# One pass over all tokens instead of two, with feature-major activations, in an eight-core decoder-trunk kernel

## The chip, the cores and the metric

The kernel runs on all 8 NeuronCores of one Trainium2 chip. Every core executes the same program on its own slice of the tokens, and the cores exchange nothing. The metric is device time in microseconds (us) of the slowest core, as the median of several executions.

## What is computed

Four layers of a hybrid decoder trunk, for a prompt of 4 x 2048 tokens and a sample group of 128 x 8 tokens. The width is 2048, and the feed-forward width 8192.

```python
def _layer(x, pool_hist, conv_hist, pos0, ...):
    proj = jnp.einsum('bld,de->ble', x, w_in)          # 2048 -> 4096
    p, u, v, gate_b, gate_c, z = jnp.split(proj, IN_SPLITS, axis=-1)
    a_out, pool_new = _pool_mixer(p, pool_hist, pos0, w_pool, pool_scale)  # trailing windows 2/4/8/16
    u = jax.nn.gelu(u)
    v = _layernorm(jax.nn.gelu(v), ln_v_g, ln_v_b)
    b_out = _spatial_gate(u, v, w_s, b_s)              # 8 heads, 128-position chunks
    conv_y, conv_new = _short_conv(gate_c * z, conv_hist, w_conv)          # width 3
    mix = jnp.concatenate([a_out, b_out, gate_b * conv_y], axis=-1)
    h = _layernorm(ALPHA * x + jnp.einsum('ble,ed->bld', mix, w_out), ln1_g, ln1_b)
    f = jnp.einsum('blf,fd->bld', jnp.square(jax.nn.relu(h @ w_ff1)), w_ff2)
    x = _layernorm(ALPHA * h + f, ln2_g, ln2_b)
```

Per token and layer the four large weight matrices hold 512 (w_in), 256 (w_out), 1024 (w_ff1) and 1024 (w_ff2) blocks of 128 x 128, together 2816. All inputs and outputs are float32 in HBM; the matmuls run in bf16.

## The kernel before

Each core owns half a sequence (1024 prompt tokens) and 128 sample tokens. A sequence is divided between two cores at position 1024, and pooling, convolution and gating look back, so a core that has a second half also computes tokens ahead of its own, which get fewer from layer to layer. The tokens are worked in tiles of 128 and in **two passes of six tiles** (`T = 768` columns). Pass 0 holds three tiles of such lead-in and three own tiles, pass 1 five own tiles and the sample tile. In pass 0 the output tiles shrink to 6, 5, 4 and 3 in layers 0 to 3. Both passes go through all four layers, so all weights are read twice, in 2 x 4 x 44 = 352 blocks of 2048 x 512 (2 MB as bf16 in SBUF). There are two slots (`wsl0`, `wsl1`). GpSimd's queue starts a block's transfer when the slot's last reader on TensorE is done, and the transfer converts fp32 to bf16.

The residual `X` stands token-major in SBUF (tokens on partitions), in fp32. A layer runs through `phase_v`, `phase_b`, `phase_a`, `phase_c`, `phase_out` and `phase_ffn`:

- Projections whose result is wanted feature-major take weights as the stationary operand and `actT` as the moving one, in groups of 256 to 512 columns (384 with six tiles). Projections that return to `X` (`w_out`, `w_ff2`, also `v`) take 128 tokens as the stationary operand and 512 weight columns as the moving one.
- ScalarE evicts the first half of the feed-forward (`relu2`: Relu into `rl`, then Square into `mixT`). VectorE adds the second half to `X`, line 352 or 362.
- A layernorm is done per tile of tokens (`ln_stats`, `ln_rstd`, `ln_apply`): `bn_stats` on four pieces of 512, then two passes of 2048 on VectorE (L362). `fm_cast` (ScalarE) makes a bf16 copy `xb`, and `fm_tr` transposes it on TensorE into `ptb` (L451), from where ScalarE copies it to `actT`. The next projection needs `actT`.
- Matmuls rotate over six PSUM banks `pb` and two banks `ptb` for transposes. Engines run in program order, and every wait is on a semaphore.

Line 340 of the profile is the helper `mm` (every matmul), 349 `act`, 352 `tt`, 356 `ts`, 362 `stt`, 99 `dma`. The loop of the feed-forward that carries most of the work reads:

```python
            for s in range(4):
                for fb in range(4):
                    ...
                    sl, sbf = w_get()
                    for e in range(4):
                        for gi in range(ngrp):
                            ...
                                mm(pt[:, 0:gw], sl[:, dc, e * 128:(e + 1) * 128], actT[:, dc, c0:c1], ...
                            relu2(mixT[:, fc, c0:c1], pt[:, 0:gw], gw, pb, mixbufs(fc, c0, c1))
                for db in range(4):
                    sl, sbf = w_get()
                    for t in tiles:
                            mm(pt[:, :], mixT[:, fc, t * 128:(t + 1) * 128], sl[:, fc, :], fc == 0, fc == 15, ...
```

## Time and profile before

| what | value |
|---|---|
| time, median of 3 runs | 8297.62 us (8265.32 to 8550.75) |
| span of the profiled execution, slowest core | 8170.0 us |
| spans of the eight cores | 8077.3 to 8170.0 us |
| TensorE busy | 6971.1 us (85%), 39048 matmuls |
| VectorE / ScalarE busy | 1810.8 us (22%) / 1655.2 us (20%) |
| HBM read | 1542.85 MB |

The span goes from the first to the last instruction on the core. The times of the runs hold what lies around it too; the profiled execution has no time of its own beside its span. The lowest of the three runs lies 95 us above this span and the median 128 us. A row on the clock gives the share of its full speed (2.4 GHz) that TensorE was granted, as a mean over a stretch.

### The profile page before, as it was taken

What the parts mean: (1) busy time and instruction counts of PE and PEld (TensorE: products, weight loads), DVE (VectorE), ACT (ScalarE), POOL (GpSimd) and SP (SyncE); (2) the same over time, 40 slices, a digit from 0 to 9 for tenths busy, and PEclk for the clock granted to TensorE, in tenths of its full rate; (3) what the DMA queues carried; (4) which work ended last, traced back from release to release, by engine and by line L of the source; (5) the groups of instructions that cost most, each with busy time, mean ns of one, the idle gap of its engine ahead of it and who ended that gap; (6) DMA issues with size and microseconds to landing.
All of it is one profiled execution on the core that took longest, in us unless ns stands there. A gap on an engine that the chain in (4) does not pass through costs nothing.

```text
span 8170.0 us, 94139 instructions; the slowest of 8 cores (8077.3 to 8170.0 us)
## 1 busy us (share of the span) xinstructions
PE 6971.1 (85%) x39048; PEld 3714.9 (45%) x39048; DVE 1810.8 (22%) x2667; ACT 1655.2 (20%) x2864; POOL 420.0 (5%) x377
## 2 busy tenths in 40 slices
PE   6899977999788866676889987899978999788998
PEld 3455544555443333333455544555434555345454
DVE  2410143101320041003320033311234100432112
ACT  3122120221211121113021221211131222212111
POOL 0000000000000000000000000000000000000000
PEclk9899988999899988888899988999989999889999
DMA  5566655788489869996567644667736788546775
GB/s 101 93 101 101 100 87 94 111 112 116 79 134 120 125 97 134 117 121 131 88 94 103 97 77 72 113 97 103 94 65 98 93 96 101 81 80 98 98 99 103
DMA packets 761119, 822.23 MB, mean 101 GB/s; under 512 B 26740, under 2 KB 748148, under 8 KB 753852
## 3 DMA queue, kind: packets, MB, share of 16 engines
q0 software_dynamic: 743264, 742.43, 65.8%
q1 hardware_dynamic: 17436, 73.77, 2.6%
q8 instruction: 317, 5.19, 0.3%
q14 instruction: 102, 0.84, 0.0%
HBM read 1542.85 MB, written 16.65 MB: 191 GB/s over the span
## 4 chain that ended last, share of the span: by engine, by line
PE 66%; DMA 19%; DVE 7%; issue 5%; ACT 3%; DVEq 0%; another core or an unknown queue 0%; ACTq 0%; POOL 0%; POOLq 0%; SPq 0%
PE pb L340 65%; DMA wsl<-w_ff 14%; DMA wsl<-w_in 3%; DVE X L362 3%; DMA wsl<-w_out 2%; DVE R L352 1%; DVE stats L424 1%; PE ptb L451 1%; ACT actT L349 1%; DVE R L362 1%; ACT L349 1%; ACT R L349 0%; ACT xb_0 L349 0%; ACT xb_1 L349 0%; DVE stats L409 0%
## 5 line engine op out<-in xcount | busy, mean ns | idle before, releaser
L340 PE MATMUL pb<-actT,wsl 128*128 128x384 bf16 (+3 forms) x21696 | 3446.9, 323 | 376.0 <-DMA wsl<-w_ff 261.5
L340 PE MATMUL pb<-wsl,mixT 128*128 128x512 bf16 x13440 | 2936.2, 381 | 106.0 <-DMA wsl<-w_ff 67.7
L340 PEld LDWEIGHTS pb<-actT,wsl 128*128 128x128 bf16 x21696 | 2061.6, 101 | 1736.3 <-issue 571.8
L340 PEld LDWEIGHTS pb<-wsl,mixT 128*128 128x128 bf16 x13440 | 1318.1, 98 | 1714.4 <-issue 155.3
L349 ACT ACTIVATE rl<-pb 128x384 f32<-128x384 f32 (+3 forms) x1008 | 456.7, 453 | 3411.8 <-PE pb L340 3411.6
L352 DVE TENSOR_TENSOR X<-pb,X 128x512 f32<-128x512 f32 x504 | 347.9, 690 | 3401.7 <-PE pb L340 3401.6
L362 DVE SCALAR_TENSOR_TENSOR X<-X,pb 128x512 f32<-128x512 f32 x336 | 230.4, 686 | 1533.8 <-PE pb L340 1533.5
L99 POOL DMA_DIRECT2D wsl<-w_ff x256 | 292.7, 1143 | 5021.6 <-PE pb L340 5001.4
L349 ACT ACTIVATE mixT<-rl 128x384 bf16<-128x384 f32 (+3 forms) x1008 | 491.9, 488 | 96.8 <-ACT rl L349 5.9
L362 DVE SCALAR_TENSOR_TENSOR X<-X,mvall,R 128x2048 f32<-128x2048 f32 x168 | 389.9, 2347 | 12.3 <-DVE mvall L433 2.9
L340 PE MATMUL pb<-wsl,actT 128*128 128x512 bf16 x1344 | 310.5, 395 | 42.6 <-DMA wsl<-w_in 42.6
L349 ACT ACT_TABLE_LOAD x100 | 128.3, 1283 | 1038.1 <-DVE mvall L426 926.2
L451 PE MATMUL ptb<-identb,xb_1 128*128 128x128 bf16 x720 | 77.4, 278 | 233.6 <-ACT actT L349 188.4
L340 PEld LDWEIGHTS pb<-wsl,actT 128*128 128x128 bf16 x1344 | 135.7, 101 | 214.4 <-issue 69.0
L424 DVE BATCH_NORM_STATS2 stats<-X 128x6 f32<-128x512 f32 x336 | 206.8, 678 | 0.0
L451 PE MATMUL ptb<-identb,xb_0 128*128 128x128 bf16 x672 | 66.7, 270 | 155.4 <-ACT xb_0 L349 94.6
L340 PE MATMUL pb<-dd,wpool_t 128*128 128x384 bf16 (+2 forms) x56 | 22.6, 492 | 203.4 <-DVE dd L362 110.0
L349 ACT ACTIVATE R<-pb 128x384 f32<-128x384 f32 (+2 forms) x204 | 109.1, 535 | 428.4 <-PE pb L340 424.9
L349 ACT ACTIVATE actT<-ptb 128x1024 bf16<-128x1024 bf16 x174 | 176.9, 1017 | 24.1 <-PE ptb L451 15.0
L451 PEld LDWEIGHTS ptb<-identb,xb_1 128*128 128x128 bf16 x720 | 61.3, 125 | 249.1 <-issue 249.0
L99 POOL DMA_DIRECT2D wsl<-w_in x64 | 73.4, 1147 | 1831.5 <-PE pb L340 1831.5
L349 ACT ACTIVATE mvall<-mvall,epst 128x3 f32<-128x3 f32 (+2 forms) x30 | 9.0, 300 | 660.3 <-DVE mvall L426 660.2
(70 smaller groups left out, 1435.5 us busy)
## 6 DMA issues: line engine op xcount, KB each, us to landing
wsl<-w_ff POOLq DMA_DIRECT2D x256, 2048.0 KB, 17.2
wsl<-w_in POOLq DMA_DIRECT2D x64, 2048.0 KB, 15.7
wsl<-w_out POOLq DMA_DIRECT2D x32, 2048.0 KB, 16.8
R<-ln_g SPq DMA_DIRECT2D x16, 1024.0 KB, 5.3
R<-ln_b SPq DMA_DIRECT2D x16, 1024.0 KB, 7.4
X<-x_in SPq DMA_DIRECT2D x12, 1024.0 KB, 18.1
y<-X SPq DMA_DIRECT2D x9, 1024.0 KB, 3.9
R<-lnv_g SPq DMA_DIRECT2D x8, 512.0 KB, 4.3
```

The lines of the kernel that those rows point to most:

```text
L99: q.h.dma_start(out=out, in_=in_).then_inc(ds.sem, 16)
L340: return op(PE, lambda: nc.tensor.matmul(out, lhsT, rhs, start=start, stop=stop), reads=reads, writes=[bank], acc=not first, force_inc=boo ...
L349: return op(ACT, lambda: nc.scalar.activation(out=out, in_=in_, func=func, **kw), reads=reads, writes=writes)
L352: return op(DVE, lambda: nc.vector.tensor_tensor(out=out, in0=in0, in1=in1, op=o), reads=reads, writes=writes)
L362: return op(DVE, lambda: nc.vector.scalar_tensor_tensor(out=out, in0=in0, scalar=scalar, in1=in1, op0=o0, op1=o1), reads=reads, writes=writes)
L424: op(DVE, lambda k=k: nc.vector.bn_stats(out=st[:, k, :], in_=X[:, t, k * 512:(k + 1) * 512]), reads=[Xb[t][k]], writes=[stb[k]])
L451: op(PE, lambda k=k, dc=dc, pt=pt: nc.tensor.transpose(pt[:, k, :], xb[:, dc * 128:(dc + 1) * 128], identb[:]), reads=[xbb, identbb], writ ...
```

## The change

The kernel is written anew around the same arithmetic.

- **One pass.** A core holds 1296 columns at once: 16 + 112 lead-in columns, 16 columns `E` (the first 16 positions of a sequence's second half, or those just before), 1024 own and 128 sample columns. Layer 0 computes 1280 of them to the end, layers 1 to 3 compute 1168 (`O_START`). The sequence is now divided at position 1040, 16 positions inside a 128-position chunk, and small extra operations handle those 16 (`before_e`, `WE`, `CBE`, `et`, `ey`).
- **Weights** are read once, in 4 x 176 = 704 blocks of 2048 x 128, stored contiguously in HBM by the host, through ten slots of one buffer `wsl` (`w_issue` after a block's last use).
- **Features on partitions throughout.** `X`, the activations `actg[g]` and `mixT` are feature-major; weights are always the stationary operand (save for `v`), and each block is applied to three token groups `g` = 2, 1, 0 of 512, 384 and 272 columns (384 in layer 0). There are no transposes. All eight PSUM banks rotate.
- **Layernorm by token groups.** While the last projection before a layernorm is evicted, `stat_acc` adds each of the 16 feature chunks to `sacc` (VectorE) and its square (ScalarE) to `qacc` (VectorE). `ln_stats` sums both over the partitions by two fp32 matmuls with a matrix of 1/2048, then computes Ln and Exp on ScalarE for the reciprocal root. 16 `items` per group (VectorE `scale`, `shift`, ScalarE gain and offset into bf16) apply it. `tail` runs the last eight blocks group by group and interleaves the items of the group before, and `head` runs the first eight blocks of the next projection group by group while the rest is applied. Gain and offset of `X` itself are not applied but folded into the next residual (`aga`).
- **SBUF** doesn't hold everything at once: mixer buffers lie in the space of `X`, which is written to HBM after the second layernorm (`xs_d`) and read back before `w_out` (`reload`, 8 transfers).
- **Input** comes feature-major in fp32, in four transfers per token group, each group after the one before, and ScalarE and VectorE convert it.

```diff
-NT = 6
-T = NT * 128
-TG = 384
 ALPHA = (2 * DEPTH) ** 0.25
 EPS = 1e-5
 WINDOWS = (2, 4, 8, 16)
-NSLOT = 2
+TIN = 1296
+XO = 16
+TX = TIN - XO
+C_T, C_E, C_OWN, C_S = 16, 128, 144, 1168
+P_START = (0, 112, 128, 128)
+O_START = (16, 128, 128, 128)
+GB = ((0, 400), (400, 784), (784, 1296))
+ORDER = (2, 1, 0)
+NWB = 176
+NSLOT = 10
...
-        def w_issue_upto(k):
-            while wstate['issue'] <= min(k, len(blocks) - 1):
-                b = wstate['issue']
-                s = b % NSLOT
-                dma(POOL, wsl[s][:], blocks[b], wsld[s], writes=[wslb[s]])
-                wstate['issue'] += 1
-
-        def w_get(hold=0):
-            b = wstate['use']
-            w_issue_upto(b + NSLOT - 1 - hold)
-            wstate['use'] += 1
-            return wsl[b % NSLOT], wslb[b % NSLOT]
-
...
-        def ln_stats(t):
-            i = ln_rot.next()
-            st, stb = stats[i], statb[i]
-            for k in range(4):
-                op(DVE, lambda k=k: nc.vector.bn_stats(out=st[:, k, :], in_=X[:, t, k * 512:(k + 1) * 512]),
-                   reads=[Xb[t][k]], writes=[stb[k]])
-            op(DVE, lambda: nc.vector.bn_aggr(out=mvall[:, t, 0:2], in_=st[:, 0:4, :].rearrange("p k s -> p (k s)")),
-               reads=stb[0:4], writes=[mvallb[t]])
-
...
-                pt, pb = ptp.next()
-                for k in range(8):
-                    dc = half * 8 + k
-                    op(PE, lambda k=k, dc=dc, pt=pt: nc.tensor.transpose(pt[:, k, :], xb[:, dc * 128:(dc + 1) * 128], identb[:]),
-                       reads=[xbb, identbb], writes=[pb], acc=(k > 0), force_inc=(k == 7))
-                act(actT[:, half * 8:(half + 1) * 8, t * 128:(t + 1) * 128], pt[:, :, :], AF.Copy, [pb], [actb[t]])
...
+        def w_issue():
+            b = wst['issue']
+            if b >= nblk:
+                return
+            s = b % NSLOT
+            dma(POOL, wsl[:, s].rearrange("p a b -> p (a b)"), wb_d[b], wds[s], writes=[wsl[:, s]])
+            wst['issue'] += 1
...
+        def fm4(places, c0, c1):
+
+            got = [banks.next() for _ in range(4)]
+            for k in range(16):
+                for i, (pt, bk) in enumerate(got):
+                    lw, rh = wsl[:, places[i], k, :], actc(k, c0, c1)
+                    mm(pt[:, 0:c1 - c0], lw, rh, k == 0, k == 15, [lw, rh], bk, k == 0)
+            return got
...
+        xin_ds = [[dsem(f"xin{g}_{q}") for q in range(4)] for g in range(3)]
+        for g in ORDER:
+            if g < 2:
+                SP.wait_for(('d', xin_ds[g + 1][3], 16))
+            for q in range(4):
+                d = xst[g][:, 4 * q:4 * q + 4, :]
+                dma(SP, d, xg_d[g][:, 4 * q:4 * q + 4, :], xin_ds[g][q], writes=[d])
...
+            if off is None:
+                tt(s_, x, s_, ALU.add, [x, s_], [s_])
+            else:
+                stt(s_, x, off, s_, ALU.add, ALU.add, [x, s_] + ro, [s_])
+            q_flush()
+            sq = sqt[g].next()[:, 0:n]
+            act(sq, x, AF.Square, [x] + ro, [sq], bias=off)
+            pend.append((q, sq))
...
+        def ln_stats(g, c0, c1):
+            n = c1 - c0
+            s_, q = sacc[g][:, 0:n], qacc[g][:, 0:n]
+            pm, bm = banks.next()
+            mm(pm[:, 0:n], onesf[:], s_, True, True, [onesf[:], s_], bm, True)
+            pq, bq = banks.next()
+            mm(pq[:, 0:n], onesf[:], q, True, True, [onesf[:], q], bq, True)
+            a, b = rn[g][0][:, 0:n], rn[g][1][:, 0:n]
+            m2 = sqt[g].next()[:, 0:n]
+            act(m2, pm[:, 0:n], AF.Square, [bm], [m2])
+            act(a, pm[:, 0:n], AF.Copy, [bm], [a])
+            tt(b, pq[:, 0:n], m2, ALU.subtract, [bq, m2], [b])
+            ts(b, b, 0.0, None, ALU.max, None, [b], [b])
+            act(b, b, AF.Ln, [b, epst[:, 0:1]], [b], bias=epst[:, 0:1], scale=1.0)
+            act(b, b, AF.Exp, [b], [b], scale=-0.5)
+            stt(a, a, -1.0, b, ALU.mult, ALU.mult, [a, b], [a])
+
...
+                def scale():
+                    if off is None:
+                        tt(x, x, b, ALU.mult, [x, b], [x])
+                    else:
+                        o_ = off(c)
+                        stt(x, x, o_, b, ALU.add, ALU.mult, [x, b, o_], [x])
+
+                def shift():
+                    tt(x, x, a, ALU.add, [x, a], [x])
+                    gg, bb = vec(l, gi + c), vec(l, bi + c)
+                    if after == 'y':
+                        act(x, x, AF.Identity, [x, gg, bb], [x], scale=gg, bias=bb)
+                    else:
+                        h = actc(c, c0, c1)
+                        act(h, x, AF.Identity, [x, gg, bb], [h], scale=gg, bias=bb)
...
+        def tail(og, src, ks, resid, accum, items, rate=(1, 1, 2), order=ORDER):
+
+            places = [w_get() for _ in range(8)]
+            prev = None
+            for gi, g in enumerate(order):
+                c0, c1 = og[g]
+                for i in range(8):
+                    pt, bk = fm(places[i], c0, c1, src, ks)
+                    if gi == 2:
+                        w_issue()
+                    now = [todo.pop(0) for _ in range(min(rate[gi], len(todo)))]
+                    for scale, _ in now:
+                        scale()
+                    resid(8 + i, g, c0, c1, pt, bk)
+                    for _, shift in now:
+                        shift()
+                    accum(8 + i, g, c0, c1)
+                    if prev is not None and i == 2:
+                        p0, p1 = og[prev]
+                        ln_stats(prev, p0, p1)
+                        todo.extend(items(prev, p0, p1))
+                q_flush()
+                prev = g
+            return prev
...
+        def head(og, sink, last, items):
+            places = [w_get() for _ in range(8)]
+            for gi, g in enumerate(ORDER):
+                c0, c1 = og[g]
+                if last is not None:
+                    drain(len(todo) - (16 if gi < 2 else 0))
+                if gi < 2:
+                    for i, (pt, bk) in enumerate(fm4(places, c0, c1)):
+                        sink(i, c0, c1, pt, bk)
+                if last is not None:
+                    drain(6)
+                for i in range(4 if gi < 2 else 0, 8):
+                    if last is not None:
+                        if gi == 0 and i == 6:
+                            p0, p1 = items[1][last]
+                            ln_stats(last, p0, p1)
+                            todo.extend(items[0](last, p0, p1))
+                        drain(3)
+                    pt, bk = fm(places[i], c0, c1, actc, K16)
+                    if gi == 2:
+                        w_issue()
+                    sink(i, c0, c1, pt, bk)
...
+            work = [lambda h=h: b_head(l, h) for h in range(8)]
+            work[3:3] = [lambda g=g: pool_map(l, g) for g in range(4)]
+            work.pop(0)()
...
+                for e in (2 * half, 2 * half + 1):
+                    for block in (c_gate, c_z):
+                        block(l, e, w_get())
+                        w_issue()
+                        work.pop(0)()
+                for j in range(2):
+                    c_out(l, 2 * half + j, w_get())
+                    w_issue()
+                    if work:
+                        work.pop(0)()
+            dma(SP, ctail_d[l], ctail[:], dd["ct_o"], reads=[ctail[:]])
...
+            for e in range(8):
+                s = w_get()
+                for g in ORDER:
+                    c0, c1 = og[g]
+                    pt, bk = fm(s, c0, c1, mixc, KW)
+                    out_resid(e, g, c0, c1, pt, bk)
+                    out_accum(e, g, c0, c1)
...
```

Three places show what stands in a row now. On TensorE, at the end of `w_out` and the start of the feed-forward in pass 0, layer 0, before (`pb<-wsl,mixT` is `w_out`, `ptb` are transposes of layernormed tiles, `pb<-actT,wsl` the first block of `w_ff1`):

```order
L340 MATMUL pb<-wsl,mixT 128x512 x384
L451 MATMUL ptb<-identb,xb_0 128x128 x16
L451 MATMUL ptb<-identb,xb_1 128x128 x16
L340 MATMUL pb<-actT,wsl 128x128 x64
L451 MATMUL ptb<-identb,xb_0 128x128 x16
L340 MATMUL pb<-actT,wsl 128x128 x64
```

And the same place now, on TensorE in layer 1 (`act_44`, `act_45`, `act_46` are the activations of groups 2, 1 and 0; `onesf` marks the two sums of `ln_stats`):

```order
L343 MATMUL pb<-mixT,wsl 128x512 x128
L343 MATMUL pb<-mixT,wsl 128x384 x48
L343 MATMUL pb<-sacc_101,onesf 128x512
L343 MATMUL pb<-qacc_102,onesf 128x512
L343 MATMUL pb<-mixT,wsl 128x384 x80
L343 MATMUL pb<-mixT,wsl 128x272 x48
L343 MATMUL pb<-sacc_103,onesf 128x384
L343 MATMUL pb<-qacc_104,onesf 128x384
L343 MATMUL pb<-mixT,wsl 128x272 x80
L343 MATMUL pb<-act_44,wsl 128x512 x96
```

The transposes and the 128-column matmuls between them are gone. The sums of a group stand three blocks behind its last matmul.

On VectorE in the third group of the same `tail` (`rnB`, `rnA` are scale and shift of group 2, `agab` the folded gain, `rnD`, `rnC` those of group 1), now:

```order
L336 SCALAR_TENSOR_TENSOR X<-X,agab,rnB 128x512 x2
L336 SCALAR_TENSOR_TENSOR X<-X,agab,pb 128x272
L327 TENSOR_TENSOR X<-X,rnA 128x512 x2
L336 SCALAR_TENSOR_TENSOR sacc_105<-X,agab,sacc_105 128x272
L327 TENSOR_TENSOR qacc_106<-qacc_106,sqt_109 128x272
L327 TENSOR_TENSOR rnD<-pb,sqt_108 128x384
L333 TENSOR_SCALAR rnD<-rnD 128x384
L336 SCALAR_TENSOR_TENSOR rnC<-rnC,rnD 128x384
```

Where VectorE had four `bn_stats` and a sum per tile, it now has an eviction of 272 columns among four passes of 512 and two sums, and the short chain of `ln_stats` in the middle.

On VectorE behind the last pooling group of layer 1, now (`ssum`, `ptmp`, `et` are the window sums, `CB` the gating bias):

```order
L327 TENSOR_TENSOR ssum_97<-ssum_96 128x1041
L327 TENSOR_TENSOR ptmp_72<-ptmp_71 128x16x8
L327 TENSOR_TENSOR et_67<-et_66 128x16
L336 SCALAR_TENSOR_TENSOR mixT<-ssum_97,pb_69 128x1024
L327 TENSOR_TENSOR tmp_61<-ssum_97,rc0t 128x15
L327 TENSOR_TENSOR mixT<-tmp_61,pb_69 128x15
L336 SCALAR_TENSOR_TENSOR mixT<-et_67,eb 128x16
L336 SCALAR_TENSOR_TENSOR mixT<-ptmp_72,histt 128x128
L336 SCALAR_TENSOR_TENSOR pb<-pb,vecs_t,CB 128x384
```

The last row evicts the first gating head. It was ahead of pooling before (`phase_b` came first) and now stands behind all of pooling's VectorE work.

## Rows read from the trace of the kernel before

**Rows 1.** Spans and clocks by core: span, mean granted TensorE clock.

```profile
core 6: 8170.0 us, clock 0.927
```

**Rows 2.** The page's chain that ended last: shares by engine, then by line.

```profile
PE 66%; DMA 19%; DVE 7%; issue 5%; ACT 3%; DVEq 0%; another core or an unknown queue 0%; ACTq 0%; POOL 0%; POOLq 0%; SPq 0%
```

**Rows 3.** TensorE's waits: who for whom, us in total, times, longest.

```profile
PE pb L340 <- DMA wsl<-w_ff: 329.2, 79, 19.1
...
PE ptb L451 <- ACT actT L349: 247.8, 63, 15.4
...
PE pb L340 <- DMA wsl<-w_in: 136.8, 15, 15.3
...
PE pb L340 <- DVE dd L362: 110.0, 16, 9.1
```

**Rows 4.** Stretches: busy by engine, then granted clock, DMA share, GB/s written.

```profile
500.00:600.00 100.00, 100.00 (x497) 48.44 (x495) 16.51 (x24) 7.10 (x14) 4.57 (x4) 1.00 0.69 105
...
4300.00:4400.00 100.00, 97.51 (x578) 56.14 (x576) 2.76 (x4) 32.47 (x64) 5.71 (x5) 1.00 0.78 100
...
4800.00:4900.00 100.00, 62.97 (x319) 31.13 (x318) 62.24 (x83) 37.91 (x37) 2.78 (x3) 0.76 0.34 57
```

**Rows 5.** The stretch 500 to 1000 us on core 4, form of Rows 4.

```profile
core 4: us, PE busy (x) PEld busy (x) DVE busy (x) ACT busy (x) POOL busy (x), PEclk, DMA share, GB/s
500.00:1000.00 500.00, 498.74 (x2674) 263.78 (x2696) 49.74 (x72) 97.17 (x192) 27.60 (x25) 1.00 0.68 101
```

**Rows 6.** Matmul groups by form, whole span: count, busy us, mean ns.

```profile
L340 PE MATMUL pb<-wsl,mixT 128*128 128x512 bf16 x13440 | 2936.2, 381 | 106.0 <-DMA wsl<-w_ff 67.7 <-DMA wsl<-w_out 35.2 <-DVE X L352 2.0
...
L340 PE MATMUL pb<-actT,wsl 128*128 128x384 bf16 x14976 | 2570.6, 335 | 256.5 <-DMA wsl<-w_ff 170.9 <-DMA wsl<-w_in 69.9 <-ACT mixT L349 8.1
...
L340 PE MATMUL pb<-actT,wsl 128*128 128x128 bf16 x2688 | 164.8, 224 | 0.8
...
L647 PE MATMUL pb<-identf,R 128*128 128x128 f32 x32 | 6.6, 289 | 19.1 <-DVE R L384 19.1
```

**Rows 7.** Matmuls by form in the stretch from 5500 to 5600 us.

```profile
L340 PE MATMUL pb<-wsl,mixT 128*128 128x512 bf16 x338 | 73.1, 379 | 0.0
```

**Rows 8.** Timeline of TensorE: start, us, form, count.

```profile
5447.00 20.96 PE L340 MATMUL pb<-actT,wsl 128*128 128x384 bf16 x128 [1.76 <-DMA wsl<-w_ff]
```

**Rows 9.** A stretch of pass 0, layer 3, in the form of Rows 4.

```profile
3300.00:3400.00 100.00, 61.41 (x304) 31.65 (x303) 2.77 (x4) 15.22 (x30) 5.72 (x5) 0.81 0.91 115
```

**Rows 10.** DMA issues: count, KB written each, median us to landing.

```profile
wsl<-w_ff POOLq DMA_DIRECT2D x256, 2048.0 KB, 17.2
...
wst<-wsTp POOLq DMA_DIRECT2D x4, 256.0 KB, 3.9
```

**Rows 11.** The first 50 us, in the form of Rows 4.

```profile
0.00:50.00 50.00, 11.19 (x96) 9.76 (x96) 3.09 (x11) 24.78 (x20) 4.83 (x9) 1.00 0.99 209
```

**Rows 12.** The chain of the start: start, us, what.

```profile
3.90 47.34 DMA wsl<-w_in
```

**Rows 13.** Timeline of VectorE at the end.

```profile
8142.26 23.65 DVE L362 SCALAR_TENSOR_TENSOR X<-X,mvall,R 128x2048 f32<-128x2048 f32 x10
```

**Rows 14.** VectorE groups by form: count, busy us, mean ns.

```profile
L352 DVE TENSOR_TENSOR X<-pb,X 128x512 f32<-128x512 f32 x504 | 347.9, 690 | 3401.7 <-PE pb L340 3401.6
...
L352 DVE TENSOR_TENSOR R<-R 128x782 f32<-128x782 f32 x32 | 30.9, 966 | 0.5 <-DVE tmst L384 0.3 <-issue 0.2
...
L352 DVE TENSOR_TENSOR R<-pb,R 128x384 f32<-128x384 f32 x48 | 26.7, 555 | 173.8 <-PE pb L340 173.4
...
L352 DVE TENSOR_TENSOR pes<-pes 128x352 f32<-128x352 f32 x16 | 8.4, 525 | 1.7
...
L356 DVE TENSOR_SCALAR R<-R,flagt 128x15 f32<-128x15 f32 x16 | 5.9, 371 | 1.7
```

**Rows 15.** ScalarE groups by form: count, busy us, mean ns.

```profile
L349 ACT ACTIVATE rl<-pb 128x512 f32<-128x512 f32 x60 | 35.8, 597 | 390.9 <-PE pb L340 390.9
...
L349 ACT ACT_TABLE_LOAD x100 | 128.3, 1283 | 1038.1 <-DVE mvall L426 926.2 <-DVE mv L411 75.0 <-PE pb L340 28.2
```

More of the change, by code:

```diff
@@ L21, with group_of, groups @@
 WINDOWS = (2, 4, 8, 16)
-NSLOT = 2
+TIN = 1296
[8 more added lines that the diff above has]
+NSLOT = 10
+NV = 96
+def group_of(c):
+    for g, (a, b) in enumerate(GB):
+        if a <= c < b:
+            return g
+def groups(start):
+    return {g: (max(a, start), b) for g, (a, b) in enumerate(GB)}
 class Eng:
@@ new lines, in vcopy, with mm @@
+        def vcopy(out, in_, reads, writes):
+            op(DVE, lambda: nc.vector.tensor_copy(out=out, in_=in_), reads, writes)
+        def mm(out, lhsT, rhs, start, stop, reads, bank, first):
+            op(PE, lambda: nc.tensor.matmul(out, lhsT, rhs, start=start, stop=stop), reads, [bank], acc=not first,
+               force=bool(stop))
+        wds = [dsem(f"wds{i}") for i in range(NSLOT)]
+        nblk = depth * NWB
+        wst = {'issue': 0, 'use': 0}
+        def w_issue():
[5 more added lines that the diff above has]
+            wst['issue'] += 1
@@ L821, in build @@
+        last, ln2 = None, None
+        for l in range(depth):
+            last, ln2 = layer(l, last, ln2)
+        drain(len(todo) - 12)
+        c0, c1 = ln2[1][last]
+        ln_stats(last, c0, c1)
+        todo.extend(ln2[0](last, c0, c1))
+        drain(len(todo))
+        for n in ("chv_o", "pl_o", "cv_o", "pt_o", "ct_o"):
+            SP.wait_for(('d', dd[n], dd[n].count))
+        for ds in y_ds:
+            SP.wait_for(('d', ds, ds.count))
     return nc
```

1374 lines of the change are left out of this document (718 added, 656 removed).

## Prediction

> **What bounds the kernel now.** I began with the core's span and the chain that ended last. TensorE holds 66% of that chain and weight transfers most of the rest, 19%; VectorE has 7% [rows 2]. So the question is how long TensorE works and for what it stands still. It is busy 6971 of 8170 us and idle 1199 us. Its longest waits are for weight blocks (329 and 137 us), for the copy that follows each transpose (248 us), and for pooling (110 us) [rows 3].
>
> Next, what full speed looks like. In the middle of the feed-forward TensorE is busy without a gap at a granted clock of 1.00, the upper level of 2.4 GHz; at a layer's end, where it is idle 37%, the mean clock is 0.76 [rows 4]. In a dense stretch 338 matmuls of 512 columns take 73.1 us, 216.3 ns each [rows 7], and 128 of 384 columns take 20.96 us, 163.8 ns each [rows 8]. A column costs (216.3 - 163.8)/128 = 0.41 ns, just 2.4 GHz. The 128-column matmuls, each with its own weight load, take 164.8/2688 = 61.3 ns [rows 6], so a weight load doesn't hold back a matmul of 272 columns; from the slope that one takes 163.8 - 112 x 0.41 = 117.9 ns.
>
> What the clock costs: at those rates (137.5 ns for 320 columns by the slope, 61.3 for a bf16 one of 128) the 39048 matmuls of before come to 6650 us, and 6971 were measured. So 1199 us of idleness brought 321 us of slower work with them, **0.27 us per idle us**.
>
> **TensorE's work after the change.** I counted the matmuls in the new program's order. 11552 of 512 columns x 216.3 = 2499 us; 13728 of 384 x 163.8 = 2249; 7872 of 272 x 117.9 = 928; 384 of 400 or 288 columns, 57; 768 of 128 columns (split `v` blocks, gating) x 61.3 = 47; pooling maps and bias sums, 12. The 48 fp32 sums of `ln_stats` have 19136 columns; a transpose of 128 fp32 columns took 6.6/32 = 0.206 us [rows 6], so they take 31 us. The sum is **5823 us**. 82 us of that are not in the four big matrices. The saving against 6650 is 827 us: tokens that were computed twice, transposes (1392), and the bias matmuls (672).
>
> **Weights.** A block is now 512 KB written and TensorE needs a new one every 216.3 + 163.8 + 117.9 = 498 ns x 16 = 7.97 us in layers 1 to 3, 8.70 us in layer 0. When the transfers were the bound (pass 0, layer 3, 64 x 163.8 ns = 10.5 us of work per 2 MB block), they moved 115 GB/s at a DMA share of 0.91 [rows 9], which is 4.6 us for 512 KB. Two sizes give another view: 256 KB landed in 3.9 us and 2048 KB in 17.2 us [rows 10]; the line through them gives 5.8 us for 512 KB, of which 2.0 are fixed. Either is below 7.97 us, and ten slots lie ahead instead of two. `head` and `tail` release eight blocks in 15 us, yet what follows needs the third new block only 14 to 16 us after the first release, and the eighth after 35 us; at 4.6 us each they come in time. The spill and `reload` of `X` (9.6 MB per layer) go beside 16 blocks of `w_out` (127 us) and fit: 25.6 MB of reads in 127 us is 202 GB/s, while 115 GB/s written of bf16 is 230 GB/s read. So the 466 us and more of weight waits [rows 3] go to nothing, and so do the transposes' 248 us. What is late next is VectorE, in two places.
>
> **The pooling stage.** On VectorE an operation of n elements took 0.525 us for 352 and 0.966 for 782, so 0.165 + 0.00102 n; the PSUM forms agree (0.690 at 512, 0.555 at 384) [rows 14]. A pooling group now has two to four sums over 1050 columns (1.24 us each), as many over 352 and 30 (0.7), a difference over 1024 (1.2) and some ten small ones (0.17 to 0.37). That is 7.4, 9.3 and 11.3 us for groups 1 to 3, with 24 bias operations (6.2) between: 34.2 us against TensorE's 3 x 7.97 = 23.9. VectorE also starts 8 us late. `b_head(0)` follows at once, and its three banks are freed only at 44 us from the start of group 1. TensorE gets as far as `b_head(1)` at 34 us, where the eight banks come round. It waits 10 us there and 2 more behind it: 12 us per layer, **48 us**. The nearest measured wait is that for pooling, 110/8 = 14 us a layer and pass; it is the upper side, and 0 the lower.
>
> **The layernorm stages.** In the third group of `tail` a block costs VectorE 3 x 0.443 + 4 x 0.690 = 4.1 us where it carries two items of group 2, and TensorE 16 x 117.9 ns = 1.9 us. In its middle stands `ln_stats`: two fp32 sums (1.6 us), two ScalarE passes (1.2), three on VectorE (1.9), Ln and Exp with table loads of 1.28 us each [rows 15], during which VectorE waits in its queue. I make it 7 us, 4 of them idle on VectorE. Followed in program order, VectorE is 9 us behind at the end of the second group, which makes TensorE's sums of that group wait 3 us, and 24 us behind at the end of the third; then `fm4`, which needs the bank of block 3, starts 8 us late. Its activation chunks then arrive faster than it needs them. So 11 us for each of seven boundaries, less in layer 0 where group 0 is wider: **75 us**. All of the lag exposed would be 24 each, none of it 0.
>
> **Start and end.** Until the first `v` matmul before, 47 us pass on a block in the chain [rows 12], while 209 GB/s are written at a share of 0.99 [rows 11]. The first group (4 MB) plus an equal read share of weights (2 MB written) is 6 MB, 29 us at that rate; the next 3 MB and four blocks take 25 more, while TensorE has 28 us of work. I take **35 us** lost. At the end 16 items of 512 columns follow the last sums, 2 x 0.690 x 16 = 22 us, plus seven items and sums ahead of them and the last write: **48 us**, where before ten passes took 23.65 us of a tail of 37 [rows 13]. Other small waits: 20 us (0 to 30).
>
> VectorE's total goes from 1811 to about 2000 us by the same line, and ScalarE's falls. Neither is near 6100, so both matter only in these stages.
>
> **The sum.** 5823 + 48 + 75 + 35 + 48 + 20 = 6049 us; 226 us of idleness bring 0.27 x 226 = 61 us of slower clock; the span is **6110 us** (8170 before [rows 1]). The median before lies 128 us above the profiled span; with as much around it, the time is **6240 us**. The low end, with VectorE's lags hidden and 95 us around it, is 5823 + 1.27 x 103 + 95 = 6049.
>
> **Rivals.** *A: VectorE's lag is exposed in full*, as the wait that takes the place of the weights': 7 x 24 instead of 75 and 4 x 20 instead of 48 are 125 us more, x 1.27 = 159, so 6400. For it speaks that the queues are strictly in order, against it that eight banks lie between.
>
> *B: TensorE, busy nearly throughout, isn't granted the full clock.* The trace speaks against it: all eight cores are dense together between 500 and 1000 us, busy 498.7 to 500.0 of 500 us, and all at 1.00 (core 4 stands in [rows 5]). But no such stretch is longer than some 600 us. If the mean fell to that of before, 0.927 [rows 1], the time is 5823/0.927 + 226 + 128 = 6636. The Trainium skill (TensorE: Matmul & The Clock Gate, the note on the peak-current limiter in Part 1) states that with three dense cores on a die the clock goes to 13/16 and stays there. These rows show the contrary for 500 us; by the page the time would be 7520.
>
> *C: the weight stream sets the pace, and the kernel is slower.* It decides at (8298 - 128)/704 = 11.6 us per block. If a transfer's time didn't scale with its bytes, 17.2 us as for a whole block of before [rows 10], one after another would give 704 x 17.2 = 12100 us. Against it: 256 KB in 3.9 us from the same queue, and rows of 4 KB where there were rows of 1 KB.
>
> *D: it doesn't read and compute less.* The order shows 704 transfers of 1 MB and 13.6 million columns instead of 15.6, so this is out.
>
> **How the numbers follow.** Forecast (6050 to 6320) 0.57, A 0.15, B 0.18 (a third of it beyond 6640), C 0.02, faster than 6050 0.08. The range that leaves out 0.16 is 6050 to 6640. Within 2%, which is what a measurement of this kernel can tell from no change, lies next to nothing: faster 0.97, same 0.01, slower 0.02.
>
> **What would show it.** The granted clock is 1.00 in most slices and TensorE above 94% busy. Matmuls of 272 columns take 118 ns. No wait for `wsl` above some us stands past the first 60 us. TensorE's waits are for VectorE, at `fm4`, at `onesf` and at gating heads 1 and 2. The prediction fails if weight loads hold back the 272-column form, if the clock stands below 1.00 in dense stretches, or if blocks land slower than one in 7.97 us.

## The result and the profile after

| | before | after |
|---|---|---|
| time, median | 8424.19 us (8225.06 to 8822.33, 6 runs) | 6246.94 us (6000.54 to 6537.8, 6 runs) |
| ratio of undisturbed runs | | 0.7265, 95% interval 0.7189 to 0.7341 |
| profiled execution: time | | 6097.67 us |
| its spans | 8077.3 to 8170.0 us | 5990.7 to 6096.6 us |

In four of the six executions of the changed kernel, and in others of the kernel before, the cores of one die or of both are granted a lower clock for part of the time (in the profiled one below, cores 4 to 7), and the median of 6246.94 us contains them; without them the changed kernel takes 6000 to 6004 us, and this is what I compare from here on, calling such executions and cores undisturbed.

So the kernel is faster by 27%, as forecast. The nearness of 6246.94 to 6240 is luck: the forecast has a span of 6110 us and 128 us around it, while the undisturbed span is 6004 us, and the time lies 1 us above the slowest core's span (6097.67 against 6096.6). The undisturbed time of 6000 to 6004 us lies below 6050, the lower end of the forecast; only the median lies inside.

The spans of the cores after (before: [rows 1]):

```profile
core 0: 6001.6 us, clock 0.986
...
core 3: 6004.2 us, clock 0.986
...
core 6: 6096.6 us, clock 0.970
```

I read core 3. The chain that ended last, by engine, was TensorE 66%, DMA 19%, VectorE 7% [rows 2]; now, on the page of the slowest core, 6:

```profile
PE 90%; DVE 4%; issue 3%; DMA 1%; ACT 1%; DVEq 0%; SPq 0%; ACTq 0%; POOLq 0%
```

Stretches of core 3, columns as in [rows 4]: the start, the feed-forward of layer 0, a stretch of 50 us with pooling, the feed-forward of layer 2, the end, and the whole span.

```profile
0.00:100.00 100.00, 62.73 (x299) 30.64 (x300) 7.89 (x17) 20.85 (x31) 6.70 (x16) 0.96 0.81 196
...
1000.00:1500.00 500.00, 500.00 (x2774) 271.29 (x2773) 59.38 (x99) 106.89 (x205) 30.61 (x58) 1.00 0.37 62
...
1790.00:1840.00 50.00, 41.90 (x229) 22.84 (x230) 31.19 (x73) 6.11 (x12) 2.17 (x5) 0.90 0.31 57
...
4000.00:4100.00 100.00, 100.00 (x607) 59.20 (x606) 0.00 (x0) 36.49 (x75) 6.33 (x12) 1.00 0.40 69
5900.00:6000.00 100.00, 56.38 (x299) 29.87 (x297) 81.28 (x163) 47.34 (x79) 0.00 (x0) 0.81 0.23 86
...
0.00:6004.00 6004.00, 5844.24 (x34508) 3360.72 (x34508) 1904.36 (x3739) 1485.27 (x2778) 374.07 (x712) 0.99 0.43 81
```

TensorE is busy 5844 of 6004 us, 97%, and idle 160 (before 6971 and 1199). In the dense stretches it stands at 1.00 without a gap: 500/2774 = 180.2 ns per matmul in layer 0, where my rates give (216.3 + 2 x 163.8)/3 = 181.3, and 100/607 = 164.7 ns in layer 2, where they give 166.0. At the DMA shares of 0.37 and 0.40 TensorE waits for no weights there.

What it still waits for, core 3, columns as in [rows 3]:

```profile
PE pb L343 <- DVE mixT L327: 28.5, 14, 6.1
PE pb L343 <- DMA wsl<-wb: 18.3, 4, 5.9
PE pb L343 <- DVE act L340: 15.9, 1, 15.9
PE pb L343 <- DVE X L336: 12.7, 4, 3.8
PE pb L343 <- DVE pb L336: 9.8, 12, 0.9
```

The waits for weight blocks fell from 501 us (329 + 137 + 35) to 18, of which 14 lie in the first 32 us (the wait of 15.9 us for `act` is the start's, for the input); those for the copies behind a transpose are gone.

### The profile page after: what moved, and what is told of

Same layout as the page of the kernel before. It is cut to its first block, busy times and chain, and to the rows that moved or that the text cites. A ratio compares the mean times of both kernels' runs of the same rounds, so it can differ in the third digit from the quotient of the medians.

```text
span 6096.6 us, 86348 instructions; the slowest of 8 cores (5990.7 to 6096.6 us)
## 1 busy us (share of the span) xinstructions
PE 5903.7 (97%) x33969; PEld 3390.3 (56%) x34508; DVE 1904.1 (31%) x3739; ACT 1484.3 (24%) x2778; POOL 374.1 (6%) x712
## 3 DMA queue, kind: packets, MB, share of 16 engines
q0 software_dynamic: 101952, 369.67, 36.2%
## 4 chain that ended last, share of the span: by engine, by line
PE 90%; DVE 4%; issue 3%; DMA 1%; ACT 1%; DVEq 0%; SPq 0%; ACTq 0%; POOLq 0%
PE pb L343 90%; DVE X L327 1%; DMA xst<-xg 1%; DVE X L336 1%; DMA wsl<-wb 0%; DVE pb L336 0%; DVE qacc L327 0%; DVE mixT L336 0%; ACT act L324 0%; DVE gcb L336 0%; ACT sqt L324 0%; DVE sacc L336 0%; DVE sacc L327 0%; ACT rnB L324 0%; DVE CBs L336 0%
## 5 line engine op out<-in xcount | busy, mean ns | idle before, releaser
L343 PE MATMUL pb<-act,wsl 128*128 128x384 bf16 (+3 forms) x16613 | 2929.1, 338 | 99.5 <-DVE pb L336 17.6
L343 PE MATMUL pb<-mixT,wsl 128*128 128x512 bf16 (+2 forms) x15108 | 2634.4, 336 | 14.2
L343 PEld LDWEIGHTS pb<-act,wsl 128*128 128x128 bf16 x16896 | 1674.8, 99 | 1347.4 <-issue 235.6
L343 PEld LDWEIGHTS pb<-mixT,wsl 128*128 128x128 bf16 x15360 | 1519.7, 99 | 1129.0 <-issue 84.3
L324 ACT ACTIVATE pb<-pb 128x384 f32<-128x384 f32 (+2 forms) x816 | 398.9, 489 | 2846.8 <-PE pb L343 2843.5
L327 DVE TENSOR_TENSOR X<-pb,X 128x384 f32<-128x384 f32 (+2 forms) x384 | 219.9, 573 | 1707.4 <-PE pb L343 1707.0
L314 POOL DMA_DIRECT2D wsl<-wb x704 | 371.8, 529 | 5574.1 <-PE pb L343 5454.7
L324 ACT ACTIVATE mixT<-pb 128x384 bf16<-128x384 f32 (+2 forms) x864 | 430.6, 502 | 156.4 <-PE pb L343 86.1
L343 PE MATMUL pb<-wsl,act 128*128 128x512 bf16 (+4 forms) x1760 | 278.9, 321 | 3.7 <-DMA wsl<-wb 3.7
L324 ACT ACTIVATE act<-X,vecs_t 128x384 bf16<-128x384 f32 (+2 forms) x336 | 221.6, 715 | 179.9 <-DVE X L327 179.5
```

What stands on the lines that cost most here:

```text
L314: q.h.dma_start(out=out, in_=in_).then_inc(ds.sem, 16)
L324: op(ACT, lambda: nc.scalar.activation(out=out, in_=in_, func=func, **kw), reads, writes)
L327: op(DVE, lambda: nc.vector.tensor_tensor(out=out, in0=in0, in1=in1, op=o_), reads, writes)
L343: op(PE, lambda: nc.tensor.matmul(out, lhsT, rhs, start=start, stop=stop), reads, [bank], acc=not first, force=bool(stop))
```

## Experiments

I compare spans of the slowest undisturbed core. After the change it is 6000 to 6004 us. Before it is 8170 us in the profiled execution, which I take, but up to 8295 in others, so differences from it are uncertain by some 100 us. The first three experiments start from the kernel before.

**1. Half of each weight block.** From the third block on, only half of it is transferred.

```diff
-                dma(POOL, wsl[s][:], blocks[b], wsld[s], writes=[wslb[s]])
+                hc = 16 if b < NSLOT else 8
+                dma(POOL, wsl[s][:, 0:hc, :], blocks[b][:, 0:hc, :], wsld[s], writes=[wslb[s]])
```

> The kernel before, but from the third block on only the first half (8 of 16 row groups) of each weight block is transferred; the other half of the slot keeps what an earlier block left, so the weights are wrong and the work of every engine is the same. Theory 1 (waits for weights cost what the trace shows, 329 + 137 + 35 = 501 us, and 0.27 us of slower clock for each): the span falls from 8170 to about 7534 us, ratio 0.92, and no wait for wsl is left beyond some us. Rival (the waits stand at places where something else comes late just behind, such as transposes): half of it or less returns, span above 7850.

7686.56 us, spans 7670 to 7686: 485 less, where 636 were expected. Core 0's waits:

```profile
PE ptb L452 <- ACT actT L350: 246.2, 60, 15.4
...
PE pb L341 <- DVE dd L363: 110.0, 16, 9.2
...
PE pb L341 <- DMA wsl<-w_in: 58.5, 12, 6.7
```

Weight waits on core 0 go from 493 us (501 on core 6) to 74, and other waits grow little (for `vtm` from 6 to 31). On core 6 TensorE's idle time falls by 412 us and its busy time by 81, 0.20 per idle us (0.22 to 0.24 on cores 3 and 0). So nearly all of the waits came back as time, with somewhat less slower clock on top than 0.27.

**2. No transposes after layernorms.** The bf16 copies and transposes go, and projections read layer 0's input throughout (`ln_inline` and `ln_tail` are called with False).

```diff
-                        pre = ln_inline(tiles, tiles.index(t), True)
+                        pre = ln_inline(tiles, tiles.index(t), False)
...
-            ln_tail(tiles, pre, True, ff1b0)
+            ln_tail(tiles, pre, False, ff1b0)
```

> The kernel before without the bf16 copies, transposes and copies to actT behind both layernorms (those of the input stay), so that all projections read the layer-0 input; the layernorm of X itself stays. Theory 1: the waits for them (248 + 95 + 43 = 386 us, x 1.27) and 1200 transposes of 61 ns go, 563 us, span 7607, ratio 0.93. Rival (weight transfers caught up during those waits, and TensorE now waits for blocks instead): less than 300 us gained, with the waits for wsl up from 501 us by 200 or more.

Spans of cores 0 to 3: 7979 to 8008, only 162 us less. Core 0:

```profile
PE pb L340 <- DMA wsl<-w_ff: 351.1, 72, 16.5
PE pb L340 <- DMA wsl<-w_in: 279.1, 17, 51.2
```

The 385 us of waits behind transposes shrink to 82, yet the waits for weights rise from 501 to 666, with this block's wait at the start of a layer in pass 1 (GpSimd, then TensorE):

```profile
4779.32 0.87 POOL L99 DMA_DIRECT2D wst<-wsTp  x1 [54.45 <-DVE WT L352]
4780.93 1.17 POOL L99 DMA_DIRECT2D wsl<-w_in  x1
4797.48 41.03 PE L340 MATMUL pb<-wsl,actT 128*128 128x512 bf16 x176 [51.24 <-DMA wsl<-w_in]
```

Three such waits, 51.2, 49.5 and 50.0 us, are 151 of the 279 us for `w_in`. Most of each is not the transfer: ahead of `wst` GpSimd's queue stands 54 us for VectorE's `WT`, which comes behind the layernorm's passes of 2048, and only then issues the block, which is used 16.6 us later. The kernel before has the same 54 us at this place, where TensorE waits for copies meanwhile and then 10 us for the block. So a third cause, VectorE's layernorm at the layer's end, stood behind these two; the change takes it away too, and no run takes it away alone.

**3. Both at once.**

```diff
+                hc = 16 if b < NSLOT else 8
...
-                        pre = ln_inline(tiles, tiles.index(t), True)
+                        pre = ln_inline(tiles, tiles.index(t), False)
...
```

> Both of the edits before together. If the two costs are independent, the gains add: 636 + 563 = 1199 us, span 6971, ratio 0.853. If each hides behind the other, the two together gain more than the sum of the single ones.

7524.41 us, spans 7476 to 7523: 647 less than before, about the sum of 485 and 162, not the 1200 expected. The waits for `w_in` are still 198.7 us, and 137 of them are the same three places (47.4, 44.4 and 44.9 us), though a block has half the bytes. So removing these two causes from the old structure gives under a third of what the change gave.

**4. Every block twice** (from here on, edits to the changed kernel).

```diff
             dma(POOL, wsl[:, s].rearrange("p a b -> p (a b)"), wb_d[b], wds[s], writes=[wsl[:, s]])
+            if b > NSLOT:
+                r = (b - 1) % NSLOT
+                dma(POOL, wsl[:, r].rearrange("p a b -> p (a b)"), wb_d[b - 1], wds[r], writes=[wsl[:, r]])
```

> The changed kernel with every weight block transferred twice into its slot (the second copy goes out with the next block's issue), so the weight stream moves twice the bytes, as before the change. Theory 1 (the prediction's 4.6 us for a block of 512 KB when transfers are the bound): 9.2 us per block against 7.97 of work, so the stream sets the pace, about 6500 us. Rival (the changed kernel's own trace: the weight queue is busy 36.2% of 6097 us for 704 blocks, 3.1 us each, since rows are four times as long): 6.3 us per block, within 1.5% of the changed kernel.

6119.17 us, spans 6098 to 6118: 114 us more, 1.9%. Core 3, first a dense stretch, then its weight waits:

```profile
4000.00:4100.00 100.00, 100.00 (x613) 59.78 (x612) 18.70 (x30) 8.06 (x17) 12.65 (x24) 1.00 0.80 135
```

```profile
PE pb L343 <- DMA wsl<-wb: 122.0, 20, 16.0
```

With 1 MB written per 7.97 us, 131 GB/s by the count, TensorE still has no gap there; its waits stand mostly in the mixer. The 733 MB are those of before (742), which had 115 GB/s at a share of 0.91 [rows 9]. So as many bytes in rows of 4 KB don't bring the 501 us back. Rows of 1 KB, as before, were not tried.

**5. 2688 more matmuls of 272 columns** (group 0 of each first feed-forward block is computed twice in layers 1 to 3).

```diff
                         pt, bk = fm(s, c0, c1, actc, K16)
+                        if l > 0 and g == 0:
+                            for k in K16:
+                                lw, rh = wsl[:, s, k, :], actc(k, c0, c1)
+                                mm(pt[:, 0:c1 - c0], lw, rh, k == 0, k == 15, [lw, rh], bk, k == 0)
```

> The changed kernel in which, in layers 1 to 3, the 16 matmuls of group 0 (272 columns) of 56 first-half feed-forward blocks per layer are issued twice into the same bank; the result is the same. 56 x 3 x 16 = 2688 matmuls more. Theory 1 (TensorE's columns are the bound, as the largest term of the prediction has it): 2688 x 117.9 ns = 317 us more, span 6000 to 6317. Rival (the weight stream or an eviction sets the pace of a block, and TensorE has slack): less than 160 us.

6351.46 us, span of core 3 6350.4: 346 us more, 129 ns each. Its row of the whole span:

```profile
0.00:6350.00 6350.00, 6163.94 (x37196) 3607.53 (x37196) 1903.00 (x3739) 1485.55 (x2778) 374.02 (x712) 0.99 0.40 77
```

Busy time grows by 319.7 us, 118.9 ns each (forecast for this form: 117.9). The other 26 us are gaps of some 4 us in 500, not in the list of waits. A column on TensorE is paid in full: the work is the bound.

**6. Eight slots instead of ten.**

```diff
-NSLOT = 10
+NSLOT = 8
```

> The changed kernel with 8 weight slots instead of 10, so that nothing is transferred ahead of the eight blocks that tail, head and v hold. Theory 1 (a block lands in some 5 us, and the third group of tail, 15 us, covers the first blocks of head): 0 to 5 us at each of 12 such places, at most 60 us. Rival (the depth is what removed the waits of before): over 200 us.

6007.18 us, spans 5981 to 6006: no change; core 3 waits 21.6 us for weights.

**7. Four blocks at a time, each twice.** After the first ten, blocks are issued only at every fourth release.

```diff
+            wst['call'] = wst.get('call', 0) + 1
+            if wst['call'] <= NSLOT:
+                todo_w = 1
+            else:
+                todo_w = 4 if (wst['call'] - NSLOT) % 4 == 0 else 0
...
+            if todo_w == 4:
+                for b in wst.get('old', []):
+                    r = b % NSLOT
+                    dma(POOL, wsl[:, r].rearrange("p a b -> p (a b)"), wb_d[b], wds[r], writes=[wsl[:, r]])
+                wst['old'] = new
```

> The changed kernel with weight transfers issued four blocks at a time (2 MB as bf16, the granule of the kernel before) and every block transferred twice (the traffic of before). The copies of a batch go out behind the next batch. Theory 1 (coarse granules with little ahead of them made the weight waits of before, not the bytes alone): waits for wsl above 300 us and a span over 6300. Rival (at rows of 4 KB the stream has enough slack whatever the granule): within 60 us of the doubled traffic alone, 6118.

6563.97 us, spans 6494 to 6563: 495 to 560 more. Core 3, first the waits, then two stretches:

```profile
PE pb L343 <- DMA wsl<-wb: 431.8, 55, 28.4
```

```profile
4000.00:4100.00 100.00, 100.00 (x609) 59.43 (x608) 23.41 (x38) 0.00 (x0) 13.22 (x25) 1.00 0.77 137
5000.00:5100.00 100.00, 68.21 (x474) 40.03 (x472) 29.18 (x54) 17.36 (x26) 4.76 (x9) 0.86 0.42 88
```

The weight waits of before are back in size, but not in place: before, 329 us of them stood in the feed-forward. Here few stand in dense stretches, where 137 GB/s still suffice, and most in the mixer and around the layernorms, where, as I read it, releases come in bursts. One more thing is in this edit: the second copy goes out for blocks that TensorE reads two to five blocks later, and by the program's order its reads wait for that copy. So the edit also takes away most of what lay ahead, and it doesn't separate traffic from depth.

**8. Gating heads one place later.** `b_head(0)` no longer precedes the loop in which each gating block is computed before its head.

```diff
-            work.pop(0)()
             for half in range(2):
```

> The changed kernel with the gating heads one place later: b_head(0) no longer runs ahead of the first c_gate but behind it, and so on, the last behind the last c_out. Theory 1 (TensorE waits for the banks of b_head(0) because VectorE is late from pooling): the waits for mixT and pb by VectorE (38 us) fall to some 10, span 5970. Rival (the lag only moves to the next operation in the queue): within 8 us of the changed kernel.

5961.93 and 5960.25 us, spans 5941 to 5961: 40 less. The place in layer 1, TensorE on core 3, after and then here (start, duration, form, count, wait ahead of it):

```profile
1788.83 0.33 PE L343 MATMUL pb<-WT,vtm 128*128 128x128 bf16 x3
...
1789.05 0.33 PE L343 MATMUL pb<-WT,vtm 128*128 128x128 bf16 x3
1795.46 0.17 PE L343 MATMUL pb<-WE,vtm 128*128 128x16 bf16 x1 [6.08 <-DVE mixT L327]
```

```profile
1792.86 0.33 PE L343 MATMUL pb<-WT,vtm 128*128 128x128 bf16 x3
1795.68 0.17 PE L343 MATMUL pb<-WE,vtm 128*128 128x16 bf16 x1 [2.48 <-DVE mixT L327]
```

And the clock there, in the same 50 us as shown of after (0.90), then the whole span:

```profile
1790.00:1840.00 50.00, 46.62 (x298) 28.10 (x296) 22.96 (x52) 8.44 (x17) 3.17 (x6) 1.00 0.30 54
```

```profile
0.00:5954.30 5954.30, 5811.08 (x34508) 3353.26 (x34508) 1901.05 (x3739) 1485.81 (x2778) 374.14 (x712) 0.99 0.42 82
```

Core 3 gains 50 us: 17 of idleness and 33 of busy time. In the 50 us that hold the long wait of each layer the granted clock was 0.90, 0.90, 0.93 and 0.93 and is now 1.00 in all four. So the slower clock around the waits cost twice what the waits did.

**9. Four blocks at a time, once each.** As 7 without the second transfer.

```diff
+                todo_w = 4 if (wst['call'] - NSLOT) % 4 == 0 else 0
```

> The changed kernel with weight transfers issued four blocks at a time (the granule of the kernel before), each block once. Granule and doubled traffic together gave 6543 to 6563 us, the doubled traffic alone 6118. Theory 1 (neither alone matters much; a burst of four blocks at 3 to 5 us each fits into four blocks of work, 32 us, when each is transferred once): waits for wsl under 80 us, span under 6080. Rival (the granule alone made the waits): waits over 200 us, span over 6200.

5996.74 us, spans 5976 to 5996: no change, 20.5 us of weight waits on core 3. Traffic alone costs 114 us, coarse steps alone nothing, both together (with the depth that 7 takes away) some 500: slack in one hides the other.

**10. Plain block order at the head of a layer.** `fm4` is replaced by four single blocks.

```diff
-                    for i, (pt, bk) in enumerate(fm4(places, c0, c1)):
+                    for i in range(4):
+                        pt, bk = fm(places[i], c0, c1, actc, K16)
                         sink(i, c0, c1, pt, bk)
```

> The changed kernel with fm4 replaced: the first four blocks of head are worked one after the other in groups 2 and 1, so that the first needs all 16 activation chunks after 3.5 us instead of 14. Theory 1 (VectorE is some 15 us late with the chunks there, and fm4 is what hides it): 5 to 10 us more at each of seven boundaries plus some 10 at the start, span 6040 to 6080. Rival (the chunks are there in time anyway): within 10 us of the changed kernel.

Spans of cores 4 to 7: 6019 to 6025, some 20 more, less than the 40 to 80 expected. Core 4:

```profile
PE pb L343 <- ACT act L324: 60.9, 23, 5.6
```

Working four blocks by chunks hides 61 us of waits for activations, but its own waits for free banks (20 us for `X`, 6.8 for `rnC`) go with it, so the net is small.

**11. One layernorm item per block in the third group.**

```diff
-        def tail(og, src, ks, resid, accum, items, rate=(1, 1, 2), order=ORDER):
+        def tail(og, src, ks, resid, accum, items, rate=(1, 1, 1), order=ORDER):
...
-            last = tail(og, mixc, K16, ff2_evict(3), ff2_accum, ln2_items, (1, 1, 1) if final else (1, 1, 2), (0, 1, 2) if final else ORDER)
+            last = tail(og, mixc, K16, ff2_evict(3), ff2_accum, ln2_items, (1, 1, 1), (0, 1, 2) if final else ORDER)
```

> The changed kernel with one layernorm item per block, not two, in the third group of tail, so VectorE lags less at its end and head starts with more items left. Theory 1 (what TensorE waits for at head is the bank of tail's block 3, held by VectorE's lag): the waits of 3.6 to 3.8 us for X at four of the boundaries fall, but head then drains more items ahead of its first activation chunks, so 0 to 10 us more per boundary, span 6000 to 6070. Rival (items are free wherever they stand): within 8 us.

5993.82 us, spans 5972 to 5993: no change beyond some 10 us. The wait of 3.78 us for block 3's bank becomes several of 1.3 to 2.8; core 3, layer 1:

```profile
2033.29 9.87 PE L343 MATMUL pb<-act,wsl 128*128 128x512 bf16 x45 [1.34 <-DVE X L336]
2044.54 1.02 PE L343 MATMUL pb<-act,wsl 128*128 128x512 bf16 x4 [1.38 <-ACT act L324]
2048.40 11.81 PE L343 MATMUL pb<-act,wsl 128*128 128x512 bf16 x41 [2.84 <-ACT act L324]
```

VectorE's backlog doesn't vanish by moving it to the other side of the boundary.

**12. Edit 8, and only four weight blocks ahead of the first input.**

```diff
-        for _ in range(8):
+        for _ in range(4):
+            w_issue()
+        POOL.wait_for(('d', xin_ds[2][3], 16))
+        for _ in range(4):
             w_issue()
```

> The changed kernel with the gating heads one place later, as before, and at the start only four weight transfers ahead of the first token group; the next four go out when it has landed. Theory 1 (input and weights share the transfer engines at the start, and weights 5 to 8 are not needed in the first 30 us): the start's 37 us of waits fall by 8 to 12, span 5948. Rival (the later weights come late in turn, and the wait moves behind the first group): within 4 us of 5958, or above.

5958.43 and 5965.73 us, the same as edit 8. On core 3 the waits of the start fall from 40.0 us in edit 8 to 34.3, where 8 to 12 us less were expected, and the longest from 15.9 to 14.7. In the first 50 us of the changed kernel the DMA share is 0.97; that the bytes of input and weights together bound the start fits this, but no run shows it. The best version found is edit 8, 0.7% below the changed kernel.

## Why the prediction was right, and where its sizes were off

**What bounds it.** This was right. Of the 2166 us between 8170 and 6004, 827 are full-clock work by the count, 1039 idleness (1199 to 160), and 300 slower clock by the balance. Experiment 5 shows that the work is paid by the column.

**TensorE's work.** 5823 us and 61 of slower clock were forecast, 5844 measured. The rates were 0.6 to 0.8% too high (181.3 against 180.2 ns, 166.0 against 164.7), which is about 40 us; that leaves some 60 us for the slower clock, though for 160 idle us instead of 226. **0.27 us per idle us** is an average and no price: the four pooling waits with what goes with them cost 2 us of work per idle us (experiment 8), the weight waits of before 0.20 (experiment 1).

**Weights.** The conclusion held, 18 us of waits. The 512 KB block landed in a median of 5.1 us, between my two figures of 4.6 and 5.8:

```profile
wsl<-wb POOLq DMA_DIRECT2D x704, 512.0 KB, 5.1
```

The reasons held only in part. I put it down to a block that takes less time than its work and to ten slots. Experiments 4, 6 and 9 show that doubling the traffic, dropping to eight slots or coarse steps is harmless or costs 1.9% when done alone; only traffic and coarse steps together, with less lying ahead (7), bring a loss of that size back. That the transposes' 248 us simply "go to nothing" is true of the whole change; in the old structure much of it only covered VectorE's layernorm and the block issued behind it (experiment 2).

**Pooling stage: 48 us forecast, 38 measured** (9.5, 12.1, 8.8 and 7.9 in the four layers). The mechanism and the place are as put: one long wait per layer (5.3, 6.1, 5.7, 4.7) at `b_head(1)`, the rest 0.2 to 1.2 each. VectorE's group in layer 1, parts of it on core 3:

```profile
1785.23 1.25 DVE L327 TENSOR_TENSOR ssum<-pb 128x1055 f32<-128x1055 f32 x1
...
1791.63 1.23 DVE L336 SCALAR_TENSOR_TENSOR mixT<-ssum,pb 128x1024 bf16<-128x1024 f32 x1
...
1793.43 0.62 DVE L336 SCALAR_TENSOR_TENSOR pb<-pb,vecs_t,CB 128x384 f32<-128x384 f32 x1
```

The large ones take the 1.24 us that the line gave. The pairs of sums over shrinking slices take 0.53, 0.50, 0.43 and 0.29 us from start to start instead of 0.7, and this group runs 9.5 us with its six small operations ahead (from 1783.92) instead of 11.3. TensorE stands at `b_head(1)` 34.0 us from its start of group 1 (1755.33), as put; the bank comes after 40.1 us instead of 44, and that is the difference of one long wait. What I didn't price is that this wait also drops the clock.

**Layernorm stages: 75 us forecast, 32 measured.** This is the term that was mis-sized, by more than twice. The boundaries cost 2.7, 0, 7.1, 4.6, 6.7, 4.4 and 6.7 us instead of 11 each. The boundary after layer 1's mixer, TensorE, then ScalarE and VectorE in `ln_stats` of the second group, core 3:

```profile
2023.64 0.88 PE L343 MATMUL pb<-sacc,onesf 128*128 128x384 f32 x2 [0.89 <-DVE sacc L336]
2025.19 0.88 PE L343 MATMUL pb<-qacc,onesf 128*128 128x384 f32 x2 [0.66 <-DVE qacc L327]
2025.91 9.43 PE L343 MATMUL pb<-mixT,wsl 128*128 128x272 bf16 x80
...
2037.35 0.70 PE L343 MATMUL pb<-act,wsl 128*128 128x512 bf16 x2 [1.79 <-ACT rnC L324]
2041.83 8.47 PE L343 MATMUL pb<-act,wsl 128*128 128x512 bf16 x26 [3.78 <-DVE X L336]
```

```profile
2036.36 0.47 ACT L324 ACTIVATE sqt<-pb 128x384 f32<-128x384 f32 x1
...
2038.06 0.61 ACT L324 ACTIVATE rnD<-rnD,epst 128x384 f32<-128x384 f32 x1 [0.85 <-DVE rnD L333]
2038.76 0.52 ACT L324 ACTIVATE rnD<-rnD 128x384 f32<-128x384 f32 x1
```

```profile
2036.93 0.56 DVE L327 TENSOR_TENSOR rnD<-pb,sqt 128x384 f32<-128x384 f32 x1 [1.14 <-ACT sqt L324]
2037.60 0.36 DVE L333 TENSOR_SCALAR rnD<-rnD 128x384 f32<-128x384 f32 x1
2039.39 0.56 DVE L336 SCALAR_TENSOR_TENSOR rnC<-rnC,rnD 128x384 f32<-128x384 f32 x1 [1.43 <-ACT rnD L324]
...
2057.84 0.44 DVE L327 TENSOR_TENSOR qacc<-qacc,sqt 128x272 f32<-128x272 f32 x1 [0.72 <-ACT sqt L324]
```

The two points are where I put them, the sums of the second group and the bank of block 3, with 1.5 us instead of 3 and 3.8 (and 1.8 ahead of it) instead of 8. One cause is in the rows: I charged the chain with two table loads of 1.28 us, and none stands there. Ln starts 0.10 us behind VectorE's result and Exp 0.09 us behind Ln's end, so VectorE idles 2.6 us in it, not 4. The chain of the first group has one load, 1.28 us at 2006.49, and there VectorE idles 2.9 us at that point alone. The whole program has 34 loads, 100 before [rows 15]:

```profile
L324 ACT ACT_TABLE_LOAD x34 | 43.6, 1283 | 43.1 <-DVE mv L720 15.0 <-DVE vtm L333 11.0 <-DMA xst<-xg 8.2
```

The lag itself came nearly as I followed it. Here VectorE's last sum of the second group ends 8 us behind TensorE's last matmul of it (2017.1), with 9 forecast, and that of the third group 23 us behind (2058.3 against 2035.2), with 24 forecast. So what I got wrong is not the lag but how much of it TensorE waits for: at its largest 7.1 us of 23. Behind the feed-forwards of layers 1 and 2 the second group's sums don't wait at all, and in layer 0 the two boundaries cost 2.7 us together, where I had counted nearly the full 11 each. By experiment 11, spreading the items otherwise changes next to nothing.

**Start and end.** 35 us forecast and 37.2 measured (15.85, 5.87, 5.68, 2.40 and 7.44), 48 and 45.4 (the last matmul ends at 5958.8). Other small waits: 20 forecast, 6.8 measured. The fp32 sums were put at 31 us and took about 41 busy us, two recorded matmuls each.

**Around the span.** 128 us were added and 1 is there. The distance from the median before to the profiled span was the spread between executions; I should have added nothing and widened the range. This error (127 us up) and the span's (106 us up, mostly layernorm stages, rates and small waits) make 233 us, and the median lies 243 us above the undisturbed time, which nothing in the sum stands for. That these cancel is luck.

**Rivals.** A didn't come: 70 us in both stages, not 248. B didn't come on cores 0 to 3: 0.986 over the span, with 1.00 in dense stretches. But it came in part on cores 4 to 7, which were granted 0.81 for some 600 us each, on 4 and 5 at their start, on 6 and 7 at their end, and whose spans are some 90 us longer. The same 100 us of core 3 and core 4:

```profile
300.00:400.00 100.00, 97.55 (x568) 53.45 (x567) 64.65 (x130) 11.66 (x21) 5.80 (x11) 1.00 0.67 164
```

```profile
300.00:400.00 100.00, 100.00 (x496) 51.19 (x495) 52.23 (x113) 9.23 (x17) 4.77 (x9) 0.81 0.41 89
```

No run shows what sets it off. The page of the Trainium skill that I cited (TensorE: Matmul & The Clock Gate, Part 1) would have 13/16, which is 0.81, for the whole of the dense work. This trace agrees with the level in those stretches and not with the duration: cores 0 to 3, as dense, kept 1.00.

C decides at 11.6 us per block, and blocks landed in 5.1. D is out: 370 MB of weights written, 742 before.

## What to carry to other kernels

Count the bound engine's work by column and by form from dense stretches; that alone placed TensorE's busy time within 1% (5823 us counted, 5844 measured). A wait is worth what it uncovers: experiment 2 took away 300 us of waits and gained 162, experiment 8 took away 17 and gained 50, so look both at what is late next and at whether the clock falls around the wait. When an engine waits for a transfer, look at when the transfer was issued and what its queue stood on before. Between buffer depth, step size and traffic, one slack covers for another: test the pair before naming one as the cause.

## What the hardware showed that I had not expected

- All eight cores, dense together, can keep the full clock: in the profiled execution of edit 8 they had a mean granted clock of 0.991 to 0.994 over 5942 to 5961 us, with 1.00 in the stretches of 500 us without waits. In the profiled execution of the changed kernel, cores 4 to 7 had 0.81 for some 600 us each.
- One wait of 4.7 to 6.1 us in a busy stretch brought the clock of the 50 us around it to 0.90 to 0.93; one of 2.5 us at the same place left it at 1.00.
- Bytes written in larger packets, from weights that now lie contiguous in HBM, cost the DMA engines less: the weight queue's 369.67 MB in 101952 packets (3.6 KB each) took 36.2% of 6096.6 us, 6.0 us per MB, and before 742 MB in packets of 1 KB took 65.8% of 8170 us, 7.2 us per MB, so that 135 GB/s flowed at a share of 0.80 where 115 had needed 0.91.
- After the table load at 2006.49, ScalarE ran Square, Copy, Ln, Exp, Identity and Relu in turn until 3081.60 without another one.
